# Seams between the blocks of a two-layer kernel: other accumulators, last chunks accumulator by accumulator, and side work a chunk later or earlier

## The reference, cut to what matters

```
layer 1: h = rms_norm(x, g_mix);  proj = h @ w_in
         oa  = attention of 8 heads (q and k normed, ALiBi, softmax)
         orr = retention of 4 heads, group norm, times silu(gr)
         merged = sigmoid(gate_a) * (oa @ w_o_attn) + sigmoid(gate_r) * (orr @ w_o_ret)
         x = x + merged @ w_out
         x = x + (silu(g) * u) @ w_ffn_out,  g, u = split(rms_norm(x) @ w_ffn_in)
layer 2: token mixer: gated linear attention (4 heads, decays) and
         differential attention (4 heads, two softmaxes), each head normed,
         concatenated, @ w_o_2, post norm, added
         feed-forward with a convolution of width 3 and gelu, post norm, added
```

## Time and profile before

| | |
|---|---|
| device time, three runs | 2848.84, 2855.87, 2858.39 us; median 2855.87 |
| the profiled execution | span 2854.9 us; its own time is not listed apart from the three runs |
| mean granted clock of TensorE | 0.992 |
| TensorE busy | 97% of the span, 13929 matmuls |
| VectorE, ScalarE, GpSimd busy | 58%, 46%, 4% |
| DMA | 178 GB/s on average |

### The profile page before, as it was taken

The page is one execution under the profiler, slowest core; times in us unless marked ns, Lnnn a source line. Parts: engine busy times, 40 slices in busy tenths (PEclk is TensorE's granted clock), DMA queues, the critical chain, the costliest instruction groups (busy, mean ns, idle before and its releaser), DMA issues.

```text
span 2854.9 us, 38768 instructions
## 1 busy us (share of the span) xinstructions
PE 2773.0 (97%) x13929; PEld 2326.5 (81%) x13929; DVE 1662.2 (58%) x1672; ACT 1324.7 (46%) x1551; POOL 122.5 (4%) x71
## 2 busy tenths in 40 slices
PE   7999999999999999999999999999889999999997
PEld 6887777787888888888888888777778888888886
DVE  4557654555555555555554555577576666666544
ACT  4435555454445444444444444545454444444443
POOL 0000000000000000000000000021000000000000
PEclk9999999999999999999999999999999999999999
DMA  6555555565555666555655655644446655555554
GB/s 214 185 184 165 160 169 162 176 197 196 190 186 170 188 187 184 185 183 185 196 193 191 188 171 152 186 125 132 142 155 186 188 185 184 184 186 191 194 193 140
DMA packets 233318, 508.57 MB, mean 178 GB/s; under 512 B 15765, under 2 KB 18037, under 8 KB 232212
## 3 DMA queue, kind: packets, MB, share of 16 engines
q1 hardware_dynamic: 231792, 500.36, 55.8%
q0 software_dynamic: 1312, 7.07, 0.7%
q10 hardware_dynamic: 132, 0.03, 0.0%
HBM read 505.31 MB, written 2.10 MB: 178 GB/s over the span
## 4 chain that ended last, share of the span: by engine, by line
PE 90%; DVE 5%; ACT 3%; issue 1%; DMA 1%; DVEq 0%; SPq 0%; ACTq 0%
PE ps L328 30%; PE ps L329 15%; PE ps L336 14%; PE ps L338 14%; PE ps L337 14%; DVE wlo L1097 2%; ACT whi L703 1%; PE ps L387 1%; DMA raw<-w_in 1%; PE ps L607 1%; DVE temp L1508 0%; DVE big L1506 0%; PE ps L420 0%; ACT big L771 0%; PE ps L483 0%
## 5 line engine op out<-in xcount | busy, mean ns | idle before, releaser
L1097 DVE TENSOR_TENSOR wlo<-raw,whi 128x1024 fp32r<-128x1024 f32 x952 | 1194.7, 1257 | 1115.9 <-ACT whi L703 1106.0
L703 ACT ACTIVATE whi<-raw 128x1024 fp32r<-128x1024 f32 x952 | 1008.5, 1060 | 1441.6 <-PE ps L338 721.0
L328 PE MATMUL ps<-hT,whi 128*128 128x512 f32 x3728 | 1324.8, 400 | 20.3 <-DVEq L1170 8.5
L329 PE MATMUL ps<-hT,wlo 128*128 128x256 f32 x3728 | 1049.3, 281 | 0.0
L328 PEld LDWEIGHTS ps<-hT,whi 128*128 128x128 f32 x3728 | 703.2, 189 | 197.3 <-DVEq L1170 10.1
L329 PEld LDWEIGHTS ps<-hT,wlo 128*128 128x128 f32 x3728 | 707.3, 190 | 0.0
L336 PE MATMUL ps<-whi,hT 128*128 128x512 f32 x1088 | 439.8, 404 | 12.9 <-DVE big L1609 7.2
L338 PE MATMUL ps<-whi,hT 128*128 128x512 f32 x1088 | 426.6, 392 | 0.0
L337 PE MATMUL ps<-wlo,hT 128*128 128x512 f32 x1088 | 425.8, 391 | 0.0
L336 PE MATMUL ps<-whi,split_e 128*128 128x512 f32 x832 | 325.5, 391 | 3.7 <-DVE resid L1324 3.7
L338 PE MATMUL ps<-whi,split_e 128*128 128x512 f32 x832 | 324.3, 390 | 0.0
(11 more groups left out here) (220 smaller groups left out, 1039.7 us busy)
## 6 DMA issues: line engine op xcount, KB each, us to landing
raw<-w_ffn_in SPq DMA_DIRECT2D x352, 512.0 KB, 3.5
raw<-w_in SPq DMA_DIRECT2D x304, 512.0 KB, 3.6
raw<-w_ffn_out SPq DMA_DIRECT2D x176, 512.0 KB, 4.0
raw<-w_o_ret SPq DMA_DIRECT2D x32, 512.0 KB, 4.7
raw<-w_out SPq DMA_DIRECT2D x32, 512.0 KB, 4.6
raw<-w_o SPq DMA_DIRECT2D x32, 512.0 KB, 3.6
raw<-w_o_attn SPq DMA_DIRECT2D x16, 512.0 KB, 4.4
resid<-x SPq DMA_DIRECT2D x2, 1024.0 KB, 7.2
```

What stands on the lines that cost most here:

```text
L328: pe.matmul(acc, whi[:, c % SLOTS, f], hT[:, kt, :, :], start=(kt == 0), stop=False)
L329: mm = pe.matmul(acc[:, 0:SEQ], wlo[:, c % SLOTS, f], hT[:, kt, 0, :], start=False, stop=(kt == KT - 1))
L703: act.activation(whi[:, c % SLOTS, :], raw[:, c % SLOTS, :], ACT.Copy).then_inc(hi_ready, 1)
L1097: dve.tensor_tensor(wlo[:, c % SLOTS, :], raw[:, c % SLOTS, :], whi[:, c % SLOTS, :].bitcast(F32), ALU.subtract).then_inc(lo_ready, 1)
```

## The change

On TensorE, the last two chunks of a block of "o2" are done accumulator by accumulator; both weight buffers are released at the end, and a new semaphore tells that the first two accumulators are done. All "o2" blocks use it.

```diff
-                for c in range(CPB):
+                for c in range(CPB if part is None else CPB - 2):
...
+                if part is not None:
+                    chunk_ready(blk, CPB - 1, turned, turned0 + CPB // 2)
+                    for hc in range(2):
+                        for t in range(NT):
+                            for c in (CPB - 2, CPB - 1):
+                                mm = rows_mm(ps[:, bank + 2 * hc + t, :], x(c), t, c,
+                                             slice(hc * 512, hc * 512 + 512), False, c == CPB - 1)
+                                if hc == 1 and t == 1:
+                                    mm.then_inc(split_used, 1)
+                        if hc == 0:
+                            mm.then_inc(part, 1)
+                    side(CPB - 2)
+                    side(CPB - 1)
```

```diff
-                    if u in LATE and c == CPB - 1:
+                    if u in LATE and c == CPB - 2:
                         pe.wait_ge(S(f"diag{u}"), 1)
                         pe.matmul(ps[:, 4, 0:SEQ], ones, scale_diag, start=True, stop=True).then_inc(S(f"scale{u}"), 1)
+                    if u in LATE and c == CPB - 1:
                         pe.wait_ge(S(f"scaled{u}"), 1)
...
-                        if k == 5:
+                        if k == 4:
                             root(u)
...
-                if k == 5:
+                if k == 4:
                     row_scale(u)
...
-                if k == CPB - 1:
+                if k == CPB - 2:
                     dve.wait_ge(S(f"scale{u}"), 1)
```

```diff
-                if c == 4:
+                if c == 5:
                     pe.wait_ge(S("a_on"), h + 1)
```

```diff
-            tall_block(base["oa"], 0, lambda c: oaT[:, c, :, :], side=turn_ret)
+            tall_block(base["oa"], 4, lambda c: oaT[:, c, :, :], side=turn_ret, free=nothing)
             pe.wait_ge(S("turned1"), KT // 2)
-            tall_block(base["oa"] + 1, 4, lambda c: oaT[:, c, :, :], whole=False)
+            tall_block(base["oa"] + 1, 0, lambda c: oaT[:, c, :, :], whole=False)
...
-                rows_block(base["or"] + n, n % 2, side=turn_merged)
+                rows_block(base["or"] + n, 2 + n % 2, side=turn_merged)
...
+            pe.wait_ge(S("turned2"), 4)
```

```diff
-                if c in (4, 5):
-                    for j in (2 * c - 8, 2 * c - 7):
-                        turn_group(4, resid, j, j, c - 3)
+                if c in (5, 6):
+                    for j in (2 * c - 10, 2 * c - 9):
+                        turn_group(4, resid, j, j, c - 4)
```

```diff
-                if c in (0, 3):
-                    t = c // 3
+                if c in (0, 4):
+                    t = c // 4
...
-                if c in (2, 5):
-                    t = c // 3
+                if c in (2, 6):
+                    t = c // 4
...
-            with pe.Fori(0, 2) as i:
-                for par in range(2):
-                    rows_block(base["gg"] + 2 * i + par, 1 - par, side=lambda c: linear_attention(c, 2 * i + par))
+            for h in range(G_HEADS):
+                def side(c):
+                    if c == 0 and h:
+                        linear_out(h - 1)
+                    linear_attention(c, h)
+                rows_block(base["gg"] + h, 1 - h % 2, side=side)
```

```diff
                 if pos == -1:
-                    for j, bank in enumerate((6, 4, 5)):
-                        turn_group(5, rows_d, j, bank, j + 1)
+                    turn_group(5, rows_d, 0, 7, G_HEADS - 1)
+                if pos == 0:
+                    linear_out(G_HEADS - 1)
+                    turn_group(5, rows_d, 1, 6, 2)
+                if pos == 2:
+                    turn_group(5, rows_d, 2, 6, 3, evicted=2)
...
                 if pos == -1:
-                    for j, bank in enumerate((6, 4, 5)):
-                        turn_group(5, j, bank, hT)
+                    turn_group(5, 0, 7, hT)
+                if pos == 0:
+                    turn_group(5, 1, 6, hT)
                     head_out(G_HEADS - 1)
+                if pos == 2:
+                    turn_group(5, 2, 6, hT)
```

```diff
+                    if k == CPB - 3:
+                        dve.wait_ge(S("o2_part"), n + 1)
+                        keep_m(n, 0)
...
                 block_done(blk)
-                for hc in range(2):
...
+                keep_m(n, 1)
```

More of the change, by code:

```diff
@@ L351, in rows_block, with tall_block @@
                     side(c)
-            def tall_block(blk, bank, x, side=nothing, turned=None, turned0=0, free=None, whole=True):
+            def tall_block(blk, bank, x, side=nothing, turned=None, turned0=0, free=None, whole=True, part=None):
                 side(-1)
@@ L620, in linear_attention, with linear_out @@
                             .then_inc(S("g_cross"), 1)
[L621 to L626, removed]
-            pe.wait_ge(S("second_in"), 16)
-            with pe.Fori(0, 2) as i:
-                for par in range(2):
-                    rows_block(base["gg"] + 2 * i + par, 1 - par, side=lambda c: linear_attention(c, 2 * i + par))
+            def linear_out(h):
+                pe.wait_ge(S("g_sT"), 3 * h + 3)
+                v = [gv[:, jt, h * SEQ:(h + 1) * SEQ] for jt in range(NT)]
+                pe.matmul(ps[:, 7, 0:SEQ], sT[:, 0:P], v[0], start=True, stop=True)
+                pe.matmul(ps[:, 7, SEQ:], sT[:, P:SEQ], v[0], start=True, stop=False)
+                pe.matmul(ps[:, 7, SEQ:], sT[:, SEQ + P:], v[1], start=False, stop=True).then_inc(S("g_o"), 1)
+            pe.wait_ge(S("second_in"), 16)
+            for h in range(G_HEADS):
[4 more added lines that the diff above has]
+                rows_block(base["gg"] + h, 1 - h % 2, side=side)
             q_h, diff, dT = temp[:, 512:1024], temp[:, 0:512], temp[:, 1024:1536]
@@ L684, in _ @@
                            turned=S("turned5") if n in (0, 2) else None, turned0=4 * (n // 2),
-                           free=last_kept(n) if n in (1, 2) else None, whole=(n == 0))
+                           free=last_kept(n) if n in (1, 2) else None, whole=(n == 0), part=S("o2_part"))
             pairs("ff2", 2 * FBLK, cols_block, first_side=turn_ahead(6, resid), turned=S("turned6"))
@@ L949, in turn_first @@
             def turn_first(k):
-                if k in (4, 5):
-                    for j in (2 * k - 8, 2 * k - 7):
+                if k in (5, 6):
+                    for j in (2 * k - 10, 2 * k - 9):
                         turn_group(4, j, j, hT, GAIN["pre2"])
-                    squares(4, resid_cols, k - 4, 512, k - 3)
+                    squares(4, resid_cols, k - 5, 512, k - 4)
             feed_in("ff", silu_gate, turn_ahead(3, GAIN["ffn"], 4, (3,)), 0)
@@ L1044, in m_cols, with keep_m @@
                 return rows_m[:, t, q * 512:q * 512 + 512]
+            def keep_m(n, hc):
+                at = n * CHUNK + hc * 512
+                act.activation(rows_m[:, 0, at:at + 512], ps[:, 2 * hc, :], ACT.Copy).then_inc(S("m_kept0"), 1)
             for n in range(4):
@@ L1051, in side @@
                         squares(7, m_cols, k - 1, 512, k)
+                    if n < 2 and k == CPB - 3:
+                        act.wait_ge(S("o2_part"), n + 1)
+                        keep_m(n, 0)
+                    if n == 3 and k == CPB - 3:
+                        squares(7, m_cols, 2, 512, 3)
                 ahead(base["o2"] + n, side, hold=(n < 2))
@@ L1054, in _ @@
                     block_done(base["o2"] + n)
-                    for hc in range(2):
-                        act.activation(rows_m[:, 0, n * CHUNK + hc * 512:n * CHUNK + hc * 512 + 512], ps[:, 2 * hc, :], ACT.Copy)\
-                            .then_inc(S("m_kept0"), 1)
+                    keep_m(n, 1)
                     held(base["o2"] + n)
-            for q in (2, 3):
-                squares(7, m_cols, q, 512, q + 1)
+            squares(7, m_cols, 3, 512, 4)
             root(7)
```

60 lines of the change are left out of this document (32 added, 28 removed).

## The result

The changed kernel takes 2835.61 us (median of 7 runs, 2827.68 to 2847.12) where the kernel before takes 2855.87: a ratio of 0.994, 95% interval 0.9922 to 0.9958. One run of this study, 3077.76 us at a granted clock of 0.845 ("Four long, then four short"), is a slow one and is left out of every range and ratio. The profiled execution took 2845.13 us with a span of 2843.3, 11.6 less than the profiled span before.

The account below looks back on a forecast made before the run. TensorE, busy 97% of the span, was taken as the bound, so only its waits and slow stretches could change. Gains of 15.15 us less losses of 13.1 gave net 2.0: 2853.9 us from 2855.87, range 2843 to 2861.

Parts of the forecast that it names:

- Row scale: Row scale one chunk earlier in four places: 0.25 us gained in three, 1.3 in the fourth, +2.0 in all.
- Head sums and banks: Head squares ending earlier, +1.3 us; new accumulator banks removing the wait from gating block into "oa", +5.4 us.
- Turns of the first feed-forward: End of first feed-forward: old wait of 1.0 us goes, new wait of 0.8 comes, net +0.3 us.
- Start of the output projection: First chunk waits on VectorE's queue: idle 4.7 us against 0.9, so -3.8, plus -1.9 for slow matmuls behind.
- Fifth chunk: Output projection's fifth chunk (chunk 4) waits for turn 2: -4.7 us, and -1.9 for a slow stretch behind.
- Rival (A): VectorE is not late, so the output projection's two new waits don't come: 2841.5 us, chance 0.19.
- Linear attention and last chunks: Linear attention's shorter waits, net +4.5 us; output projection's last chunks by accumulator, +0.5 and +1.15 at two seams.
- the masked sum's wait of 0.6: In two linear-attention blocks VectorE's masked sum comes late and TensorE waits 0.6 us: -1.2 us.
- the first seam: Output projection's first seam between blocks: waits of 2.0 us before, 0.95 and 0.7 now, taken as +0.5.
- "ff2": Seam from output projection into second feed-forward: last squares start 3.5 us after the end instead of 2.7, -0.8 us.
- Rival (C): TensorE stays at the lower clock through the output projection's first four chunks: slower, 2861.8 us, chance 0.09.
- Rival (B): Row scale hides fully, waits at chunk 6 included: 6.4 us more gain, 2847.5 us, chance 0.07.

Follow-up runs that it names:

- Four long, then four short: Changed kernel with column blocks doing four 512-column products, then four 256-column ones, instead of alternating: 2842.71 us, ratio 0.9971.
- the pair with the pace held: Kernel before and changed kernel, each with column-block matmuls ordered long, long, short, short: 2844.37 and 2835.66 us, ratio 0.9969.

## Why the prediction was wrong

**The wrong step** is the first one: "in steady work a matmul of 512 columns starts every 0.2265 us", and with it the sum made "against the profiled span". The step is right for row blocks. For the 58 column blocks, nearly half of the span, the profile shows one draw of two paces and not a duration of the kernel; the two are 8.5 us apart in each feed-forward. The three times of before, 2848.84 to 2858.39, were 9.6 us apart, as much as one such step, and the text took the spread for noise of 0.3%. A range of 2843 to 2861 around 2853.9 could not hold that. Of the 20 us measured, 8.7 are the change; by the forecast's own base that would have been 2847.2, inside the range. The rest is how the sections of both kernels fell: over all runs the difference is 10.8.

**The second** wrong step is the row scale's term, +2.0: the change itself gives 8.7, not 2.0, and this term is most of the difference. Term by term:

- Row scale, +2.0 forecast. Waits 3.0 (0.3, 0.5, 0.5, 1.7), the working was right: "wait 2.1 us there" came as 1.9, and 1.3 in the fourth place as 1.7. Missing was the low-clock stretch of 1.55 us behind 9 of 16 of the old waits. The forecast priced such stretches behind waits of 3.7 and more and took shorter ones as free of them. This term came to 6.1 by the mean, 4.1 more than forecast.
- The Trainium skill, "ScalarE: Activation LUTs", section "What ACT_TABLE_LOAD costs", would have added a drain of 1.38 us to the load; the text kept the row, and in the changed kernel the load at 40.20 ends at 41.48 and the root starts at 41.49. No run here shows the drain: in all 16 profiles most of the 52 loads have less than 0.1 us of idle time around them, and the measurement decides.
- Head sums and banks, +6.7: 6.85. Both right, with the 1.55 behind the wait.
- Turns of the first feed-forward, +0.3: +0.6. The new wait is 0.43, not 0.8.
- Start of the output projection: 4.7 was forecast for the idle time; 4.27 came. Fifth chunk: 4.7 forecast, 4.01 came. The slow stretches, 1.9 each: 2.85 and 1.7. The forecast saw this loss where it is, from the order of VectorE's queue alone, and undoing the edit for that one head gave it back. Rival (A), 0.19, in which the two waits don't come, fell, although the measured time is nearer to its 2841.5 than to the forecast. A time that suits a rival doesn't show its mechanism.
- Linear attention and last chunks, +4.5 and +1.65: the masked sum's wait of 0.6 didn't come, and the first seam gained 1.0, not 0.5 (the forecast's own figures, 2.0 before and 0.95 and 0.7 now, make 0.35). With the slow stretches behind them the last chunks are worth some 2.7 with "ff2", not 0.85. The section with all of the new waits lost 5.4 in the unheld profiles, against the 7.0 of the sum. In the pair with the pace held it lost 3.2, in part because before's profile has a low-clock stretch there (from 1989 to 1993 us) that the unheld one hasn't. A single profile therefore gives this term to 2 us only. "ff2" lost 0.77, forecast 0.8.
- Rival (C), a clock that stays low through four chunks: after the first wait the granted clock is back at 1.00 in 6.2 us, after the second in 4.2. Its price was mis-worked too: 2.0 / 0.2 is 10 slow matmuls, not 14. Rival (B), no wait on the row scale: 6.3 us of it stayed.

What stays open: what draws the pace. The row scale, the banks and a product in front of the section did not fix it, and the same program fell differently in two sets of runs, which were on two chips; whether the chip has a part in it, no run separates. Both feed-forwards at the short pace would put before at some 2840 (2856.7 for the profiled run, less 17) and the changed kernel at 2828 (2845.1 less 17): 6 of before's 84 times lie below 2843 (4 of the 18 in the last set, 2 of the 66 ahead of it), and of the changed kernel's 4 of the first 13 below 2831 and 1 of the next 12. Whether the change makes the short pace commoner or those 13 were a draw, no run separates.

## What to carry to other kernels

Before pricing seams, count the work between them in two stretches and two executions of the same kernel: where the counts differ at the same clock, no single profile is a base, and the spread of the times is a step and not noise. Alternating long and short matmuls had two paces here, equal ones next to each other had one; hold the pace by such an order before comparing changes of less than a per cent. When a queue with a fixed order gets more in one slot, add up its rows to the next thing that the bound engine needs: that gave two 4 us waits within 0.7 us.

## What was not expected of the hardware

- Alternating 512- and 256-column matmuls with a weight load each run at 22.19 or 22.61 us per 128 matmuls, held for a whole section of up to 22 blocks, at a granted clock of 1.00 and with no wait of TensorE between them. Four and four: 22.45; pairs: 22.29 to 22.33. Five pairs of the short pace are 1.74 us, of the long one 1.77.
- A stretch at 1.2 GHz behind a wait of 2 us comes in some executions and not in others, and so does the one at the start of linear attention, where TensorE had no such wait: it moved two sections compared here by 1.6 us. Behind waits of 4 us it came each time looked at, and cost 1.55 to 2.9 us.
